# Scores behind the transposition, remainders in halves, X awaited by half, and GLA's first heads behind the root

## What is computed

```python
# first block
h = h + 0.5 * rms(swiglu(rms(h, g), w_gate, w_up, w_down))        # f1
q, k, v, xp, g_attn, g_pool = split(rms(h, g) @ w_in)             # mix
s = q_row . k_window * 64**-0.5 + bias; o = softmax(s) @ v        # 8 heads, 4 rows of 64
m = (sigmoid(g_attn) * (o @ w_br_attn) + sigmoid(g_pool) * (pool(xp) @ w_br_pool)) @ w_out
h = h + rms(m)
h = h + 0.5 * rms(swiglu(...))                                    # f2
h = h + rms((p @ w_proj) * sigmoid(rms(h, g) @ w_gate))           # pp, pg
# second block, h = ln(alpha * h + ...) at each step
swiglu (a0); gla mixer; swiglu (a1); swiglu (b0); retention mixer; swiglu (b1)
# gla: o = chunked linear attention, 4 heads of 256 columns
out = (rms_head(o) * norm_g * silu(r)) @ w_out
```

## Time and profile before

| | us |
|---|---|
| median of 3 runs (1653.59 to 1655.48) | 1654.85 |
| the profiled execution, own time | 1656.87 |
| its span, first to last instruction | 1655.1 |
| busy in the span: PE / DVE / ACT | 1626.3 / 950.5 / 773.8 |

### The profile page before, as it was taken

The page is one execution under the profiler, slowest core; times in us unless marked ns, Lnnn a source line. Parts: engine busy times, 40 slices in busy tenths (PEclk is TensorE's granted clock), DMA queues, the critical chain, the costliest instruction groups (busy, mean ns, idle before and its releaser), DMA issues.

```text
span 1655.1 us, 18383 instructions
## 1 busy us (share of the span) xinstructions
PE 1626.3 (98%) x7782; PEld 1344.4 (81%) x7782; DVE 950.5 (57%) x931; ACT 773.8 (47%) x810; POOL 78.5 (5%) x99
## 2 busy tenths in 40 slices
PE   8999999899999999999999999999999999999998
PEld 6888887688888878888977888888888897878886
DVE  6555455576555575446558655475445556585453
ACT  6444445645434574343654444254342435454440
POOL 0121000000000000001010000000000141000000
PEclk9999999999999999999999999999999999999999
DMA  9766464366655666554555656566564654566560
GB/s 305 212 178 222 155 234 128 102 205 209 192 163 193 213 216 190 166 197 137 209 161 187 211 154 214 179 217 190 165 206 161 219 179 131 200 223 184 155 221 31
DMA packets 221921, 306.74 MB, mean 185 GB/s; under 512 B 8768, under 2 KB 144064, under 8 KB 221712
## 3 DMA queue, kind: packets, MB, share of 16 engines
q1 hardware_dynamic: 216944, 290.02, 53.9%
q0 software_dynamic: 4320, 14.95, 2.9%
q10 hardware_dynamic: 576, 0.59, 0.1%
HBM read 304.49 MB, written 1.05 MB: 185 GB/s over the span
## 4 chain that ended last, share of the span: by engine, by line
PE 88%; DVE 5%; ACT 4%; issue 2%; DMA 1%; ACTq 0%; DVEq 0%
PE bank L636 26%; PE bank L638 26%; PE bank L637 26%; PE bank L605 3%; ACT hiw L1089 2%; DVE low L1453 2%; PE bank L650 2%; PE bank L652 2%; PE bank L653 2%; ACT pr L1250 0%; DVE xn L1510 0%; DVE pr L1684 0%; DMA h<-in_x 0%; DMA raw<-in_w_in 0%; DVE st L1688 0%
## 5 line engine op out<-in xcount | busy, mean ns | idle before, releaser
L1453 DVE TENSOR_TENSOR low<-raw,hiw 128x2048 fp32r<-128x2048 f32 (+1 forms) x285 | 631.3, 2222 | 417.6 <-ACT hiw L1089 417.2
L1089 ACT ACTIVATE hiw<-raw 128x2048 fp32r<-128x2048 f32 (+1 forms) x281 | 521.9, 1865 | 366.8 <-DMA raw<-in_ffn_w_out 88.9
L636 PE MATMUL bank<-hiw,xh 128*128 128x512 f32 x1408 | 558.3, 397 | 6.0 <-DVE low L1453 2.8
L638 PE MATMUL bank<-hiw,xl 128*128 128x512 f32 x1408 | 549.4, 390 | 0.0
L637 PE MATMUL bank<-low,xh 128*128 128x512 f32 x1408 | 548.5, 390 | 0.0
L636 PEld LDWEIGHTS bank<-hiw,xh 128*128 128x128 f32 x1408 | 264.4, 188 | 65.8 <-issue 4.4
L638 PEld LDWEIGHTS bank<-hiw,xl 128*128 128x128 f32 x1408 | 264.2, 188 | 56.5
L637 PEld LDWEIGHTS bank<-low,xh 128*128 128x128 f32 x1408 | 264.7, 188 | 52.3
L636 PE MATMUL bank<-hiw,th 128*128 128x512 f32 x528 | 207.1, 392 | 0.0
L638 PE MATMUL bank<-hiw,tl 128*128 128x512 f32 x528 | 205.7, 389 | 0.0
L637 PE MATMUL bank<-low,th 128*128 128x512 f32 x528 | 205.5, 389 | 0.0
(11 more groups left out here) (238 smaller groups left out, 1131.9 us busy)
## 6 DMA issues: line engine op xcount, KB each, us to landing
raw<-in_ffn_w_in SPq DMA_DIRECT2D x176, 512.0 KB, 4.9
raw<-in_ffn_w_out SPq DMA_DIRECT2D x40, 1024.0 KB, 5.0
raw<-in_ret_w_in SPq DMA_DIRECT2D x24, 1024.0 KB, 5.1
raw<-in_ffn_w_gate SPq DMA_DIRECT2D x43, 512.0 KB, 4.3
raw<-in_ffn_w_up SPq DMA_DIRECT2D x43, 512.0 KB, 5.5
raw<-in_ffn_w_down SPq DMA_DIRECT2D x20, 1024.0 KB, 5.0
raw<-in_w_in SPq DMA_DIRECT2D x16, 1024.0 KB, 5.8
raw<-in_gla_w_in SPq DMA_DIRECT2D x12, 1024.0 KB, 5.1
```

What stands on the lines that cost most here:

```text
L636: pe.matmul(o[:, :], a, whi[:, k, :], start=start and k == 0, stop=False, skip_group_check=True)
L638: ins = pe.matmul(o[:, :], b, whi[:, k, :], start=False, stop=end, skip_group_check=True)
L1089: act.activation(hiw[s][:, 0:n], raw[s][:, 0:n], ACT.Copy).then_inc(hi.mark(i), 1)
L1453: dve.tensor_tensor(low[s][:, c0:c1], raw[s][:, c0:c1], hiw[s][:, c0:c1].bitcast(F32), ALU.subtract).then_inc(lo.mark(*what), 1)
```

## The change

- `halved`: besides tiles 0 and 1, the late tiles of all edges get their remainder in two halves of k, and `pe_pass` waits for each half in front of its blocks of k. Their high parts stay whole.
- `pe_lead` waits for half 0 of X at n = 0 and for half 1 at n = 1.
- The edges into a1 and b1 have counts (1, 2, 1) in place of (1, 3, 0): one tile goes from mid to late.
- Mixer: scores(1) stands between the passes of unit 0, and scores(u+2) behind turn(u), on all three engines.
- GLA: on DVE the heads 0 and 1 of t = 0 are scaled right behind the root, the other two behind the next low; ACT takes one hiw ahead of the squares, and copies the second transposed half before the squares of t = 1.

```diff
--- before.py
+++ after.py
@@ -341,11 +341,12 @@
         to_pg = edge(2, "pg", "rms", (5, 6), 4.0, "f2d", (2, 1, 3))
         to_a0 = edge(3, "a0", "ple", (7,), 1.0, "pg", (1, 2, 1))
         to_gla = edge(4, "gla", "ln", (8, 9), 0.5, "a0d", (3, 0, 1))
-        to_a1 = edge(5, "a1", "ln", (10, 11), 1.0, "go", (1, 3, 0))
+        to_a1 = edge(5, "a1", "ln", (10, 11), 1.0, "go", (1, 2, 1))
         to_b0 = edge(6, "b0", "ln", (12, 13), 0.5, "a1d", (3, 0, 1))
         to_ret = edge(7, "ret", "ln", (14, 15), 0.5, "b0d", (3, 0, 1))
-        to_b1 = edge(8, "b1", "ln", (16, 17), 1.0, "ro", (1, 3, 0))
+        to_b1 = edge(8, "b1", "ln", (16, 17), 1.0, "ro", (1, 2, 1))
         to_out = edge(9, "out", "ln", (18, 19), 0.5, "b1d", (0, 0, 0))
+
         edges = [to_mix, to_f2, to_pg, to_a0, to_gla, to_a1, to_b0, to_ret, to_b1, to_out]
 
 
@@ -392,6 +393,8 @@
             while j + 1 < NT and j < i + 5 and freed_by[j + 1] <= i - 2:
                 j += 1
             return j
+
+        halved = {0, 1}.union(*(e.late for e in edges))
 
         gain_src = [None] + [A[n][0:1, :] for n in ("ffn1_post_g", "mix_pre_g", "mix_post_g", "ffn2_pre_g",
                                            "ffn2_post_g", "ple_pre_g", "ple_post_g")]
@@ -624,10 +627,10 @@
         def pe_pass(pe, i, S, k0, t, o, start, stop):
 
             whi, wlo = weight(i)
-            if t == 0 and i >= 2:
+            if t == 0 and i not in halved:
                 pe_split(pe, i)
             for k in range(tiles[i].k):
-                if i < 2 and t == 0 and k in (0, 2):
+                if t == 0 and i in halved and k in (0, 2):
                     if i == 0 and k == 2:
                         pe_turn_in(pe, 1)
                     pe.wait_ge(lo.sem, lo.of(i, "first") if k == 0 else lo.of(i))
@@ -653,9 +656,6 @@
                     ins = pe.matmul(o, wlo[:, k, cols], xh[:, k0 + k, :], start=False, stop=end, skip_group_check=True)
             ins.then_inc(passed.mark(i, 1), 1)
 
-        def pe_x_ready(pe, nx, t):
-            pe.wait_ge(turn_lo.sem, turn_lo.of("x", nx, t, 1))
-
         def pe_lead(pe, stage, four, nx=None):
             for t in range(2):
                 for n, i in enumerate(four):
@@ -665,8 +665,8 @@
                         pe_turn_x(pe, nx, 0)
                     if stage == "pg" and n == 0:
                         pe.wait_ge(fn.sem, fn.of("pp", 0, t))
-                    if n == 0:
-                        pe_x_ready(pe, stage, t)
+                    if n < 2:
+                        pe.wait_ge(turn_lo.sem, turn_lo.of("x", stage, t, n))
                     if (t, n) == (0, 2) and stage == "a1":
                         pe.wait_ge(vec.sem, vec.of("s", "a1", 1, 1))
                     pe_pass(pe, i, X, 4 * (n % 2), t, PAIRS[n // 2][t], n % 2 == 0, n % 2 == 1)
@@ -798,10 +798,12 @@
                         if a == 0 and n >= 2:
                             pe.wait_ge(fn.sem, fn.of("mg", n - 2, t))
                         pe_pass(pe, at["mg"][2 * n + a], X, 4 * a, t, PAIRS[n % 2][t], a == 0, a == 1)
-                        if t == 0 and 2 * n + a < 7:
-                            scores(2 * n + a + 1)
+                        if n + a + t == 0:
+                            scores(1)
                     u = 2 * n + a
                     turn(u)
+                    if u < 6:
+                        scores(u + 2)
                     if u in (2, 4, 6):
                         attend(u // 2 - 1)
 
@@ -1269,8 +1271,6 @@
                 for a in range(2):
                     u = 2 * n + a
                     act_high(act, ahead(at["mg"][u]))
-                    if u < 7:
-                        scores(u + 1)
                     if a == 1:
                         for t in range(2):
                             dst = half((ga if n < 2 else gpo)[:, t, :], n % 2)
@@ -1353,15 +1356,15 @@
             act_high(act, ahead(at["gr"][1]))
             gate_silu(0, 0)
             gate_silu(0, 1)
+            act_high(act, ahead(at["gr"][2]))
             squares(0)
             root(0)
-            act_high(act, ahead(at["gr"][2]))
             act_high(act, ahead(at["gr"][3]))
             gate_silu(1, 0)
             gate_silu(1, 1)
             act_turned(act, ("go", 0, 0), goh[:, 0:4, 0:P])
+            act_turned(act, ("go", 1, 0), goh[:, 4:8, 0:P])
             squares(1)
-            act_turned(act, ("go", 1, 0), goh[:, 4:8, 0:P])
             root(1)
             act_high(act, at["go"][3])
             for n in range(2):
@@ -1448,7 +1451,7 @@
 
 
         def dve_low(dve, i, c0, c1, what):
-            dve.wait_ge(hi.sem, hi.of(*what))
+            dve.wait_ge(hi.sem, hi.of(*what) if i < 2 else hi.of(i))
             s = slot[i]
             dve.tensor_tensor(low[s][:, c0:c1], raw[s][:, c0:c1], hiw[s][:, c0:c1].bitcast(F32),
                               ALU.subtract).then_inc(lo.mark(*what), 1)
@@ -1459,7 +1462,7 @@
                 i = fed["lo"]
                 fed["lo"] += 1
                 n = tiles[i].k * tiles[i].width
-                if i < 2:
+                if i in halved:
                     if i:
                         dve_low(dve, i, 0, n // 2, (i, "first"))
                     dve_low(dve, i, n // 2, n, (i,))
@@ -1802,9 +1806,9 @@
                 dve.reciprocal(st[:, 72 + 12 * t:76 + 12 * t], st[:, 68 + 12 * t:72 + 12 * t]).then_inc(
                     vec.mark("gr", t), 1)
 
-            def scaled(t):
+            def scaled(t, n):
                 dve.wait_ge(vec.sem, vec.of("gr", t))
-                for hd in range(4):
+                for hd in (2 * n, 2 * n + 1):
                     o = OUT_GLA[t][hd // 2][:, (hd % 2) * 256:(hd % 2) * 256 + 256]
                     x = gr[:, t, hd * 256:hd * 256 + 256]
                     if hd % 2 == 0:
@@ -1817,12 +1821,14 @@
             masked(1)
             dve_lows(dve, ahead(at["gr"][2]))
             root(0)
+            scaled(0, 0)
             dve_lows(dve, ahead(at["gr"][3]))
-            scaled(0)
+            scaled(0, 1)
             for n in range(2):
                 dve_turned(dve, ("go", n, 0), goh[:, 4 * n:4 * n + 4, 0:P], gol[:, 4 * n:4 * n + 4, 0:P])
             root(1)
-            scaled(1)
+            scaled(1, 0)
+            scaled(1, 1)
             dve_lows(dve, at["go"][3])
             for n in range(2):
                 dve_turned(dve, ("go", n, 1), goh[:, 4 * n:4 * n + 4, P:2 * P], gol[:, 4 * n:4 * n + 4, P:2 * P])
```

## The result

| | before | after |
|---|---|---|
| median (lowest to highest), 4 runs each | 1655.16 (1653.59 to 1656.15) us | 1634.60 (1633.88 to 1634.99) us |
| profiled execution: own time, span | 1656.87, 1655.1 us | 1634.48, 1632.7 us |
| granted clock over the span | 0.995 | 0.999 |

The ratio is 0.9876, with a 95% interval of 0.9859 to 0.9893: 20.6 us faster by the medians. Predicted were 1633.9 us and a range of 1630.5 to 1640.5.

The account below looks back on a forecast made before the run. TensorE, busy 98% of the span, was taken as the bound, so only its waits and slow-clock stretches could be won. Terms 10.9 + 4.1 + 0.6 + 0.6 + 1.9 + 1.4 + 1.5 = 21.0, from median 1654.85: 1633.9 us, range 1630.5 to 1640.5.

Parts of the forecast that it names:

- Gates and attention, 10.9: Attention beside the gates, units 0 to 7: new order makes TensorE the bound, 72.6 us become 61.7, gain 10.9.
- the ring: Mixer before: ACT hiw, DVE low, logits, maximum, ACT exp, sigmoids, pT copy, then next hiw; 17.10 us for two units.
- ScalarE's pair, 14.2: Mixer: in the new order ACT's even and odd unit together take some 14.2 us, below TensorE's 14.7.
- its rival 15.9: Mixer: left-out hand-offs of 0.1 to 0.2 bring ACT's two units to 15.9, 4.2 us back, 1638; chance 0.12.
- The table switch: Mixer, ACT: a table load before the sigmoid taken as 1.28 us, against about 2.66 by the skill's rule with drain.
- the rival of 1642: Mixer: table switches cost their drain too, two units on ACT take 17.0 us, 8 back, 1642; chance 0.03.
- GLA, 4.1: GLA: first two scaled heads come right behind the root, TensorE's wait and slow stretch go; gain 4.1, bounds 2 and 4.4.
- slow stretch gone: 1.6: GLA: the stretch at the lower clock behind TensorE's wait for the scaled heads disappears, 1.6 us.
- mix, 0.6, and f2, 0.6: Edges mix and f2: halved lows let passes start earlier, xl is late next; gain 0.6 us each.
- pg and a0, 1.9: Edges pg and a0: passes start on half of the low, 0.83 us earlier at the first; gain 1.9 together.
- a1 and b1, 1.4 and 1.5: Edges a1 and b1: one low fewer before the layer norm, wait for h goes; gain 1.4 and 1.5 us.
- The slower rival: Mixer: the ring closes through TensorE, in series within a unit, 39 us lost, 10 won elsewhere, 1684; chance 0.02.

## Why the prediction was right, point by point

**The sum.** 21.0 us were predicted. The table gives 21.5 without the start of the kernel, measured from the profile with the long slow stretch; against the two other profiles of the kernel before, the stretch of the gates gains 10.4 in place of 11.4 and GLA some 0.2 less, 20.4 in all. The medians say 20.6. Of the difference of 22.4 between the two profiled executions, 0.9 is the start, and some 1.1 the length of slow stretches. That the single number came within 0.7 us is partly luck: the prediction took its price for the slow stretches from a profiled execution 2.0 us slower than the median and subtracted it from the median, 1.0 too much by the two other profiles, and took the unit 0.06 too long, eight times, which makes up for half of that. Two of its side sums are off without touching the forecast: eight times 4.8 is 38 and not 39, and the waits of the complete list (21.3) with the two slow stretches (4.1) are 25.4, not 25.8.

**Gates and attention, 10.9.** The largest term, and right: 10.4 to 11.4 in the profiles, 10.0 by the medians of the gates alone. The unit was 6.74 us in place of 6.80, which makes the stretch 61.2 in place of 61.7. The waits came as named: one of 0.64 (0.7 predicted) for the first logits, none for pT, none ahead of the branch, where the first sigmoid ends at 308.86 and its bank is wanted at 309.86. The reason was right as well: with exp put back, the ring is back. The term put the clock's part at the 2.6 of one profile; 1.6 to 2.5 is what three show.

**ScalarE's pair, 14.2, and its rival 15.9.** It takes 14.18. The first rival was made of hand-offs that the rows do not have.

**The table switch.** A load of 1.28 us starts 0.01 after the hiw before it ends, and the sigmoid follows it at 284.16, 0.02 after its end; the same holds for the load before exp. The Trainium skill (ScalarE: Activation LUTs, What ACT_TABLE_LOAD costs) adds a drain of some 1.4 us to each switch. The trace disagrees here, and the rival of 1642 falls.

**GLA, 4.1.** Measured 4.27, and 4.1 against the other profiles. The heads are done at the root + 1.1 and are wanted 3.7 later. The step that holds less well than it looks is "slow stretch gone: 1.6" (1.5 where the prediction reads the window, 1.7 start to start): with the gates alone changed, the same wait had no slow stretch. Some of what the table books to GLA would have come with the gates' part in that run, and only 2.6 is surely the wait's. That either engine's move alone does most of it was not in the prediction.

**mix, 0.6, and f2, 0.6.** 0.4 to 0.8 in the profiles taken with this code at mix, 0.5 at f2. xl is what is late, as said, by 0.31 and 0.80 us in the list of waits. The prediction's 0.3 to 0.5 was right for mix and too low for f2, where ScalarE's table load (1.28) stands between root and xh. At f2 the kernel before had two waits for xl, 0.42 at t = 0 and 0.77 at t = 1; the first is gone, and the second is as long as it was.

**pg and a0, 1.9.** 2.04. The halves carry it: without them 1.7 are lost at a0.

**a1 and b1, 1.4 and 1.5.** 1.47 and 1.48, gone with the counts put back. What is late next is the low moved behind, by 0.3 us start to start, as said.

**The slower rival** (a ring through TensorE, 1684) needed ScalarE and VectorE two units behind. They keep up: the pair on ScalarE is 0.35 us shorter than TensorE's, and in unit 7 ScalarE waits 0.84 us for TensorE's pass. With a look-ahead of one unit in place of two the stretch is the same (61.07), so the margin was larger than the prediction gave it.

**Stays open:** why the clock fell behind a stand of 2.40 us in GLA in three profiles and did not in a fourth, and why the slow stretch has different lengths. A change that alters the stand's length alone was not tried. The kernel with exp first has three stands and was profiled once, without a slow stretch; whether its slower runs had one is not shown.

## What to carry to other kernels

On an engine that works in order, look in the chain of waits for a ring that runs through two engines in turn while each idles beside the other, and ask which instruction can be put behind work of its own that nobody waits for yet; here one move of exp, with the other two engines already in the new order, was worth 8 to 9 us of 1655, while a second unit of look-ahead was worth nothing. Where a busy engine waits for a large operand, hand it over in halves, and put the tiny instruction on which another engine waits (a sum of 0.15 us) between the halves. Then look one stage on: the 0.6 us gained at pg were lost again at a0. Cost a fall of the clock behind a stand as a range from several profiles of the same kernel, not as the number of one.

## What the runs showed of the hardware

- **The clock behind a stand of TensorE.** By the list of waits, a stand of 2.98 us was followed by the lower level of 1.2 GHz in three profiles of three, one of 2.40 in three of four, and the three stands of 2.0 to 2.7 in the one profile with exp put back (6.8 us together) were not. The length of the slow stretch behind the stand of 2.98 was 3.65, 3.74 and some 5.2 us.
- **Table loads** on ScalarE took 1.28 us, with 0.01 to 0.02 between them and their neighbours where these had nothing to wait for.
- **The start of the kernel** varies: the first pass on X began between 15.66 and 17.21 us in the profiles, whatever the kernel, with waits of 0.2 to 1.9 for two small DMAs. So a difference of up to 1.5 us between two single executions can be the start alone.
